# Second mixer of a two-layer decoder trunk: adaLN steps moved off the first units of two projections, two quarters of the out-projection's input made at other times

## Chip, cores and metric
The kernel runs on 1 core of one Trainium2 chip. The metric is the device time of one execution in microseconds (us). Before the change it is 2801.41 us, the median of 3 runs (2799.87 to 2802.63).

## What is computed
A trunk of two layers works on 256 tokens of width 2048, with a vector `c` of width 2048 that modulates every sub-layer (adaLN). Cut to what matters here, where layer 1 is the second layer:

```
c_act = silu(c)
for i in range(2):
    sh1, sc1, g1, sh2, sc2, g2 = split(c_act @ ada_w[i] + ada_b[i], 6)      # 2048 x 12288 weights a layer
    h = x * (1 + sc1) + sh1
    y = mixer_ab(h, ...) if i == 0 else mixer_cd(h, ...)
    x = layer_norm(ALPHA * x + (1 + g1) * y, ln1_g[i], ln1_b[i])
    h = x * (1 + sc2) + sh2
    y = (silu(h @ w_gate[i]) * (h @ w_up[i])) @ w_down[i]
    x = layer_norm(ALPHA * x + (1 + g2) * y, ln2_g[i], ln2_b[i])

mixer_cd: gb, gc, xc, q, k, v = split(h @ w_in)          # 2048 x 6144
          yc = gb * causal_dwconv(gc * xc, conv_w)       # 3 taps, 1024 channels
          yd = diff_attention(q, k, v, ...)              # 4 heads of 2 x 128
          return concatenate([yc, yd]) @ w_out           # 2048 x 2048
```

## The kernel before
**Products.** Everything is held transposed, features on the 128 partitions and the 256 tokens along the free side. Each matrix product is a list of *units*. A unit is 512 rows by 512 columns of a weight matrix, 1 MB. SyncE's queue (SP) loads it into one of four slots of `raw` (L1690), ScalarE (ACT) copies it, rounded, into `whi` (L1724), and VectorE (DVE) subtracts the two into `wlo` (L2021). Both work in two halves, and `whi` and `wlo` have two places, so the split of unit u+2 waits until TensorE (PE) has used unit u. The activation is split in the same way into `ahi` and `alo`. PE then runs three matmuls for each pair of tiles (hi x hi, lo x hi, hi x lo: L2499, L2501, L2503), 48 a unit. Four units, one for each quarter of the 2048 rows, make a group of 512 columns; the groups alternate between two halves of PSUM.

The products of the second mixer are `in1a` (k, v and q columns: 3 bodies of 8 units, the first written out, the others a loop), `in1b` (the other columns: 24 units, written out) and `out1` (the out-projection: 16 units, whose quarters are taken in the order 2, 3, 0, 1: first the two that attention makes, then the two of the short convolution).

**Order.** Each engine's program is written out by hand, and each works through it in order. The function `product` has one version for each of DVE, ACT and PE, and calls `before` and `after` at each unit j. DVE's version does, at unit j: the steps of the adaLN sum that the table `ADA_AT` (L50) names for this j, then `before`, then the split of unit u+2 (`split_lo`), then the evacuation of a finished group, then `ada_take` where `ADA_TAKE` (L66) says so, then `after`. For a product named in `BEHIND_NORM` (L53), in the body that is written out, `before` comes ahead of the steps, and these go by `ADA_BEHIND_NORM` (L54) where it has an entry for the product's shape.

**adaLN steps.** The modulation of later sub-layers is summed beside the products. A *step* is one load of 512 rows by 512 columns of `ada_w` (1 MB, issued by GpSimd, POOL, L1637) into one of two slots of `ada_units`, and four DVE instructions that add its four tiles, scaled by `c_act`, to `ada_acc` (L2000, L2003). A load is issued when its slot has been used. Four steps make a block; PE then adds over the partitions with four small matmuls (`ada_sum`, L2466) behind the unit that `ADA_SUM` (L65) names, and DVE takes the result (`ada_take`, L2009). The tables have a row for each shape of product: `(2, 8)` is `in0u` and the bodies of `in1a`, `(2, 16)` is `out1`.

**Head of in1a.** It stands behind a layer normalisation. `ln_finish` makes the first two quarters of the new activation; the rest is done at units 0 to 2 of in1a through `before` (`ln_rest`, L1840 and L2187). At unit 0 DVE subtracts, multiplies and makes `y` for the third quarter (L2136, L2141, L2147), at unit 1 it makes the third quarter of `alo` (L2154) and subtracts and multiplies for the fourth; ACT then makes eight tiles, the fourth quarter of `ahi` and `y` (L1848, L1851), and at unit 2 DVE makes the last quarter of `alo`.

**From in1b to out1.** Attention has 6 steps for each of its 4 heads, one after each unit of in1b (`attention_act`, `attention_dve`, `attention_pe`). The last result of a head is written at its step 4 by DVE (L1494). The short convolution is eight tiles of five DVE instructions (`short_conv`, L1420); four stand beside in1b (after units 13, 15, 17, 19) and four behind it. Behind in1b, `mixed_act` (L1410) waits until PE has used all units of in1b, since the mixed result goes into the same `ahi`, and copies the four quarters; `mixed_dve` (L1502) makes `alo` for three quarters, then the last four convolutions, then the last quarter. PE waits in out1 for one quarter of `alo` after the other (`mix_lo`, L2693). In out1, PE's `ln_shift` (L2571, matmul L2575) behind unit 4 waits for a sum `y` that DVE makes from the first finished group (L2076, L2077).

Of the kernel before, what the change touches and what calls it, by code (L numbers as in the profile page):

```python
# [6 lines left out]
F32 = mybir.dt.float32  # L7
F32R = mybir.dt.float32r
ALU = mybir.AluOpType
ACT = mybir.ActivationFunctionType  # L10
# [18 lines left out]
UK = 4  # L29
HALVES = 2  # L30
# [20 lines left out]
          (1, 12): [1, 1, 0, 1, 1, 0, 0, 0, 0, 0, 0, 0], (2, 8): [1, 1, 1, 1, 1, 1, 2, 0],  # L51
          (2, 16): [1, 1, 1, 1, 0, 1, 1, 1, 0, 0, 0, 1, 0, 0, 0, 0]}
BEHIND_NORM = ("up00", "up10")  # L53
ADA_BEHIND_NORM = {(1, 8): [0, 0, 0, 1, 1, 1, 1, 0]}  # L54
ROUNDS = HT // 2
# [8 lines left out]
            4: dict(shift=4, s=5, c01=5, c23=6, sq0=7, sq1=9, S=9, q01=10, S2=12, sq2=13, q2=14, root=14, fold=14)}  # L64
ADA_SUM = {(1, 8): {7: 0}, (1, 12): {6: 0}, (2, 8): {4: 0, 7: 1}, (2, 16): {4: 0, 12: 1}}  # L65
ADA_TAKE = {(1, 8): {7: 0}, (1, 12): {7: 0}, (2, 8): {5: 0, 7: 1}, (2, 16): {5: 0, 13: 1}}  # L66

# [181 lines left out]
def build(nc, x, c, ada_w, ada_b, ln1_g, ln1_b, ln2_g, ln2_b, ffn_w_gate, ffn_w_up, ffn_w_down,  # L249
# [7 lines left out]
    by_name = {p["name"]: p for p in products}  # L257

    ctx = ExitStack()
    with ctx:  # L260
# [23 lines left out]
        ahi = sb("act_hi", [P, KT, L], F32R)  # L284
        alo = sb("act_lo", [P, KT, L], F32R)
# [60 lines left out]
        tile_used = sem("tile_used")  # L346
# [43 lines left out]
        scd = Steps(sem("sc_dve"), "m c0 c1 c2 g", start=1)  # L390
        mix_hi, mix_lo = sem("mix_hi"), sem("mix_lo")
        da_setp, da_setd = Steps(sem("da_set_pool"), "nd"), Steps(sem("da_set_dve"), "gain prod lam")
        da_sete, da_seta = Steps(sem("da_set_pe"), "sum"), Steps(sem("da_set_act"), "exp")
        dad = Steps(sem("da_dve"), "s0 s1 mx0 mx1 ng r rl t0 t1 c0 c1 rr n")
# [981 lines left out]
        HEAD_UNITS = 6  # L1376

        def attention_act(act, i, j):
            h, step = j // HEAD_UNITS, j % HEAD_UNITS

            def done(ins):
# [27 lines left out]

        def mixed_act(act):  # L1410
            act.wait_ge(tile_used, HALVES * by_name["out1"]["u0"])
            for n, src in enumerate((pr1[:, Q:Q + 4], pr1[:, Q + 4:Q + 8], pr1[:, 0:4], pr1[:, 4:8])):
                if n < 2:
                    act.wait_ge(dad.sem, dad.at(2 * n + 1, "n"))
                else:
                    act.wait_ge(scd.sem, scd.at(4 * (n - 2) + 3, "g"))
                k = UK * by_name["out1"]["order"][n]
                act.activation(ahi[:, k:k + 4], src, ACT.Copy).then_inc(mix_hi, 1)

# [22 lines left out]
        def attention_dve(dve, i, j):  # L1442
            h, step = j // HEAD_UNITS, j % HEAD_UNITS

            def done(ins):
# [51 lines left out]
            if j in (13, 15, 17, 19):  # L1497
                if j == 13:
                    dve.wait_ge(grp_done, by_name["in1b"]["g0"] + 3 + 2)
                short_conv(dve, (j - 13) // 2)  # L1500

        def mixed_dve(dve):  # L1502
            def low(n, src):
                k = UK * by_name["out1"]["order"][n]
                dve.wait_ge(mix_hi, n + 1)
                dve.tensor_tensor(alo[:, k:k + 4], src, ahi[:, k:k + 4].bitcast(F32), ALU.subtract).then_inc(mix_lo, 1)
            low(0, pr1[:, Q:Q + 4])
            low(1, pr1[:, Q + 4:Q + 8])
            low(2, pr1[:, 0:4])
            dve.wait_ge(grp_done, by_name["in1b"]["g0"] + 6 + 2)  # L1510
            for t in range(4, 8):
                short_conv(dve, t)
            low(3, pr1[:, 4:8])

# [205 lines left out]
        def _(act):  # L1720
# [239 lines left out]
            product(by_name["in1b"], take(beside), after=lambda i, j: attention_act(act, i, j))  # L1960
            mixed_act(act)
            product(by_name["out1"], None, before=ln_before(2), hold=True)
            ln_finish(2)
# [15 lines left out]
        def _(dve):  # L1979
# [471 lines left out]
            dve.wait_ge(ln_gb, 8)  # L2451
            product(by_name["out1"], into_x_last(2), before=ln_before(2), hold=True)
            ln_finish(2)
# [328 lines left out]
```

## Time and profile before

| | |
|---|---|
| median of 3 runs | 2801.41 us |
| the profiled execution | 2800.32 us, span 2798.7 us |
| mean granted TensorE clock | 0.947 |
| PE busy | 2559.9 us, 91% |
| weight loads of PE | 2317.1 us, 83% |
| DVE busy | 2057.1 us, 74% |
| ACT busy | 1215.4 us, 43% |
| GpSimd busy | 197.3 us, 7% |
| chain that ended last | PE 80%, DVE 12% |

The span runs from the first to the last instruction on the core. The busy shares are means over the whole span; what a stretch is bound by is seen in the views of that stretch. A row of the timeline has start and duration in us, the engine, the line of the kernel, the operation, what it writes and reads, how many instructions are merged (x), and in brackets how long the engine had been idle and which instruction ended that.

### The profile page before, as it was taken

How to read it: one execution, taken by the hardware profiler on the slowest of the kernel's cores; microseconds unless marked ns; L12 is line 12 of the kernel's file. 1: busy time of each engine (PE TensorE's matmuls, PEld its weight loads, DVE VectorE, ACT ScalarE, POOL GpSimd, SP SyncE). 2: the span in 40 equal slices, each digit the busy share in tenths (PEclk: the TensorE clock that was granted, in tenths of full speed). 3: DMA queues.
4: the chain of work that ended last, by engine and by line, in shares of the span. 5: the costliest groups of instructions: out<-in, count | busy, mean ns of one | idle time of the engine just before them, and what ended most of it. 6: DMA issues, size and time to landing. Idle time of an engine off the chain costs nothing.

```text
span 2798.7 us, 42169 instructions
## 1 busy us (share of the span) xinstructions
PE 2559.9 (91%) x16532; PEld 2317.1 (83%) x16532; DVE 2057.1 (74%) x2594; ACT 1215.4 (43%) x1606; POOL 197.3 (7%) x226
## 2 busy tenths in 40 slices
PE   1199999888889999999999999998999999999998
PEld 1197888777887899889988889998978898899887
DVE  7788999778488777777777898568787655555556
ACT  0145556544345443444344453453454434443444
POOL 0002232100000000000001011000000000000000
PEclk6589999888899999999999999999999999999998
DMA  9863444465447888878888489555668655555552
GB/s 336 290 238 134 151 151 158 159 203 166 143 151 272 281 274 278 283 276 284 275 284 273 169 309 356 173 166 191 231 213 284 237 193 186 194 186 194 193 188 83
DMA packets 281178, 616.00 MB, mean 220 GB/s; under 512 B 23211, under 2 KB 23746, under 8 KB 280770
## 3 DMA queue, kind: packets, MB, share of 16 engines
q1 hardware_dynamic: 248386, 488.04, 51.3%
q0 software_dynamic: 32640, 125.84, 12.7%
q8 instruction: 108, 1.77, 0.2%
q14 instruction: 44, 0.36, 0.0%
HBM read 611.73 MB, written 2.10 MB: 219 GB/s over the span
## 4 chain that ended last, share of the span: by engine, by line
PE 80%; DVE 12%; issue 4%; ACT 2%; SPq 1%; DMA 1%; DVEq 0%; POOL 0%; ACTq 0%
PE groups L2499 12%; PE groups L2503 12%; PE groups L2501 12%; PE groups L2491 11%; PE groups L2495 11%; PE groups L2493 11%; PE pc L2668 1%; PE pb L2658 1%; DVE w_lo L2021 1%; PE pm L2466 1%; SPq L1644 1%; DVE ada_acc L857 1%; DVE ada_acc L2003 1%; PE groups L1116 1%; DVE xT L2141 1%
## 5 line engine op out<-in xcount | busy, mean ns | idle before, releaser
L1724 ACT ACTIVATE w_hi<-w_raw 128x1024 fp32r<-128x1024 f32 x776 | 817.0, 1059 | 1213.3 <-PE groups L2495 543.6
L2021 DVE TENSOR_TENSOR w_lo<-w_raw,w_hi 128x1024 fp32r<-128x1024 f32 x749 | 909.1, 1223 | 547.5 <-ACT w_hi L1724 543.8
L2491 PE MATMUL groups<-w_hi,act_hi 128*128 128x512 f32 x1408 | 553.5, 393 | 21.1 <-DVE act_lo L2154 21.1
L2499 PE MATMUL groups<-act_hi,w_hi 128*128 128x256 f32 x1776 | 517.5, 291 | 40.0 <-DVE act_lo L2154 13.5
L2495 PE MATMUL groups<-w_lo,act_hi 128*128 128x512 f32 x1408 | 550.1, 391 | 0.0
L2493 PE MATMUL groups<-w_hi,act_lo 128*128 128x512 f32 x1408 | 549.8, 390 | 0.0
L2501 PE MATMUL groups<-act_lo,w_hi 128*128 128x256 f32 x1776 | 509.4, 287 | 0.0
L2503 PE MATMUL groups<-act_hi,w_lo 128*128 128x256 f32 x1776 | 508.9, 287 | 0.0
L2499 PEld LDWEIGHTS groups<-act_hi,w_hi 128*128 128x128 f32 x1776 | 348.1, 196 | 52.4 <-issue 44.2
L2499 PE MATMUL groups<-hid_hi,w_hi 128*128 128x256 f32 x1392 | 388.1, 279 | 0.0
L2503 PE MATMUL groups<-hid_hi,w_lo 128*128 128x256 f32 x1392 | 386.6, 278 | 0.0
L2501 PE MATMUL groups<-hid_lo,w_hi 128*128 128x256 f32 x1392 | 386.6, 278 | 0.0
L2003 DVE SCALAR_TENSOR_TENSOR ada_acc<-ada_units,c_act,ada_acc 128x512 f32<-128x512 f32 x450 | 337.9, 751 | 19.2 <-DMA ada_units<-in_ada_w_dram 6.2
L2501 PEld LDWEIGHTS groups<-act_lo,w_hi 128*128 128x128 f32 x1776 | 348.4, 196 | 0.2
L2503 PEld LDWEIGHTS groups<-act_hi,w_lo 128*128 128x128 f32 x1776 | 347.9, 196 | 0.0
L2491 PEld LDWEIGHTS groups<-w_hi,act_hi 128*128 128x128 f32 x1408 | 265.7, 189 | 77.7 <-DVE act_lo L2154 23.6
L2495 PEld LDWEIGHTS groups<-w_lo,act_hi 128*128 128x128 f32 x1408 | 265.4, 188 | 55.9
L2493 PEld LDWEIGHTS groups<-w_hi,act_lo 128*128 128x128 f32 x1408 | 265.7, 189 | 54.3
L2501 PEld LDWEIGHTS groups<-hid_lo,w_hi 128*128 128x128 f32 x1392 | 263.0, 189 | 0.1
L2503 PEld LDWEIGHTS groups<-hid_hi,w_lo 128*128 128x128 f32 x1392 | 261.6, 188 | 0.0
L2499 PEld LDWEIGHTS groups<-hid_hi,w_hi 128*128 128x128 f32 x1392 | 261.3, 188 | 0.1
L1637 POOL DMA_DIRECT2D ada_units<-in_ada_w_dram x120 | 90.2, 751 | 1627.8 <-DVE ada_acc L2003 1373.6
(428 smaller groups left out, 2514.4 us busy)
## 6 DMA issues: line engine op xcount, KB each, us to landing
ada_units<-in_ada_w_dram POOLq DMA_DIRECT2D x120, 1024.0 KB, 6.5
w_raw<-in_ffn_w_gate_dram SPq DMA_DIRECT2D x88, 1024.0 KB, 5.2
w_raw<-in_ffn_w_up_dram SPq DMA_DIRECT2D x88, 1024.0 KB, 5.1
w_raw<-in_ffn_w_down_dram SPq DMA_DIRECT2D x88, 1024.0 KB, 5.1
w_raw<-in_cd_w_in_dram SPq DMA_DIRECT2D x48, 1024.0 KB, 5.3
w_raw<-in_ab_w_in_dram SPq DMA_DIRECT2D x40, 1024.0 KB, 5.8
ada_units<-in_ada_w_dram SPq DMA_DIRECT2D x80, 512.0 KB, 4.5
ada_first<-in_ada_w_dram SPq DMA_DIRECT2D x24, 1024.0 KB, 9.6
```

The lines of the kernel that those rows point to most:

```text
L857: last = dve.scalar_tensor_tensor(total, unit, cact[:, k:k + 1], total, ALU.mult, ALU.add)
L1116: pe.matmul(dst, whi[:, j % 2, kk, cols], ahi[:, k], start=(q == 0 and kk == 0 and t % 2 == 0), stop=False, skip_group_check=True)
L1637: engine.dma_start(aw[:, j % 2], src[UK * P * j:UK * P * (j + 1), bass.ds(col, GROUP)] .rearrange("(k p) n -> p k n", p=P)).then_inc(lande ...
L1724: act.activation(whi[:, half, k], raw[:, slot, k], ACT.Copy).then_inc(hi_done, 1)
L2003: last = dve.scalar_tensor_tensor(acc[:, b], unit[:, kk], cact[:, k:k + 1], acc[:, b], ALU.mult, ALU.add)
L2021: dve.tensor_tensor(wlo[:, half, k], raw[:, slot, k], whi[:, half, k].bitcast(F32), ALU.subtract).then_inc(lo_done, 1)
L2491: pe.matmul(dst, hi[:, k, rows], whi[:, j % 2, kk], start=(k == 0), stop=False, skip_group_check=True)
L2493: pe.matmul(dst, lo[:, k, rows], whi[:, j % 2, kk], start=False, stop=False, skip_group_check=True)
L2495: last = pe.matmul(dst, hi[:, k, rows], wlo[:, j % 2, kk], start=False, stop=(k == UK * p["units"] - 1), skip_group_check=True)
L2499: pe.matmul(dst, whi[:, j % 2, kk, cols], hi[:, k], start=(q == 0 and kk == 0 and n % 2 == 0), stop=False, skip_group_check=True)
L2501: pe.matmul(dst, whi[:, j % 2, kk, cols], lo[:, k], start=False, stop=False, skip_group_check=True)
L2503: last = pe.matmul(dst, wlo[:, j % 2, kk, cols], hi[:, k], start=False, stop=(q == p["units"] - 1 and kk == UK - 1), skip_group_check=True)
```

## The change
Four things are changed.

1. `in1a` joins `BEHIND_NORM`, and `(2, 8)` gets a row in `ADA_BEHIND_NORM`: in the written-out body of in1a, the normalisation's rest comes ahead of the steps, and the steps are 0, 0, 1, 1, 2, 2, 2, 0 for its eight units where they were 1, 1, 1, 1, 1, 1, 2, 0.
2. For shape `(2, 8)` sum and take of the first block are one unit later. This holds for in0u and all bodies of in1a.
3. In out1 the steps go from 1, 1, 1, 1, 0, 1, ... to 0, 0, 2, 1, 1, 1, ...; its sums and takes stay where they were.
4. The first mixed quarter of out1 is made during in1b, at unit 22 (ACT's copy and DVE's subtraction). Of the four convolutions behind in1b, two stay in front of out1 and two go behind unit 0 of out1, with the last quarter's copy and subtraction.

```diff
-          (2, 16): [1, 1, 1, 1, 0, 1, 1, 1, 0, 0, 0, 1, 0, 0, 0, 0]}
-BEHIND_NORM = ("up00", "up10")
-ADA_BEHIND_NORM = {(1, 8): [0, 0, 0, 1, 1, 1, 1, 0]}
+          (2, 16): [0, 0, 2, 1, 1, 1, 1, 1, 0, 0, 0, 1, 0, 0, 0, 0]}
+BEHIND_NORM = ("up00", "in1a", "up10")
+ADA_BEHIND_NORM = {(1, 8): [0, 0, 0, 1, 1, 1, 1, 0], (2, 8): [0, 0, 1, 1, 2, 2, 2, 0]}
-ADA_SUM = {(1, 8): {7: 0}, (1, 12): {6: 0}, (2, 8): {4: 0, 7: 1}, (2, 16): {4: 0, 12: 1}}
-ADA_TAKE = {(1, 8): {7: 0}, (1, 12): {7: 0}, (2, 8): {5: 0, 7: 1}, (2, 16): {5: 0, 13: 1}}
+ADA_SUM = {(1, 8): {7: 0}, (1, 12): {6: 0}, (2, 8): {5: 0, 7: 1}, (2, 16): {5: 0, 12: 1}}
+ADA_TAKE = {(1, 8): {7: 0}, (1, 12): {7: 0}, (2, 8): {6: 0, 7: 1}, (2, 16): {6: 0, 13: 1}}
@@ -1375,8 +1375,12 @@
         MQ = 51
         HEAD_UNITS = 6
 
+        MIX_AT = 22
+
         def attention_act(act, i, j):
             h, step = j // HEAD_UNITS, j % HEAD_UNITS
+            if j == MIX_AT:
+                mixed_act(act, 0)
 
             def done(ins):
                 ins.then_inc(daa.sem, 1)
@@ -1407,15 +1411,15 @@
                 on(dae_, "ss")
                 done(act.activation(dastd[:], pb[:, L:2 * L], ACT.Sqrt, scale=1.0 / (2 * P), bias=consts[:, 0:1]))
 
-        def mixed_act(act):
-            act.wait_ge(tile_used, HALVES * by_name["out1"]["u0"])
-            for n, src in enumerate((pr1[:, Q:Q + 4], pr1[:, Q + 4:Q + 8], pr1[:, 0:4], pr1[:, 4:8])):
-                if n < 2:
-                    act.wait_ge(dad.sem, dad.at(2 * n + 1, "n"))
-                else:
-                    act.wait_ge(scd.sem, scd.at(4 * (n - 2) + 3, "g"))
-                k = UK * by_name["out1"]["order"][n]
-                act.activation(ahi[:, k:k + 4], src, ACT.Copy).then_inc(mix_hi, 1)
+        def mixed_act(act, n):
+            src = (pr1[:, Q:Q + 4], pr1[:, Q + 4:Q + 8], pr1[:, 0:4], pr1[:, 4:8])[n]
+            act.wait_ge(tile_used, HALVES * (by_name["out1"]["u0"] - (1 if n == 0 else 0)))
+            if n < 2:
+                act.wait_ge(dad.sem, dad.at(2 * n + 1, "n"))
+            else:
+                act.wait_ge(scd.sem, scd.at(4 * (n - 2) + 3, "g"))
+            k = UK * by_name["out1"]["order"][n]
+            act.activation(ahi[:, k:k + 4], src, ACT.Copy).then_inc(mix_hi, 1)
 
         def short_conv(dve, t):
 
@@ -1441,6 +1445,8 @@
 
         def attention_dve(dve, i, j):
             h, step = j // HEAD_UNITS, j % HEAD_UNITS
+            if j == MIX_AT:
+                mixed_low(dve, 0)
 
             def done(ins):
                 ins.then_inc(dad.sem, 1)
@@ -1499,18 +1505,23 @@
                     dve.wait_ge(grp_done, by_name["in1b"]["g0"] + 3 + 2)
                 short_conv(dve, (j - 13) // 2)
 
+        def mixed_low(dve, n):
+            src = (pr1[:, Q:Q + 4], pr1[:, Q + 4:Q + 8], pr1[:, 0:4], pr1[:, 4:8])[n]
+            k = UK * by_name["out1"]["order"][n]
+            dve.wait_ge(mix_hi, n + 1)
+            dve.tensor_tensor(alo[:, k:k + 4], src, ahi[:, k:k + 4].bitcast(F32), ALU.subtract).then_inc(mix_lo, 1)
+
         def mixed_dve(dve):
-            def low(n, src):
-                k = UK * by_name["out1"]["order"][n]
-                dve.wait_ge(mix_hi, n + 1)
-                dve.tensor_tensor(alo[:, k:k + 4], src, ahi[:, k:k + 4].bitcast(F32), ALU.subtract).then_inc(mix_lo, 1)
-            low(0, pr1[:, Q:Q + 4])
-            low(1, pr1[:, Q + 4:Q + 8])
-            low(2, pr1[:, 0:4])
+            mixed_low(dve, 1)
+            mixed_low(dve, 2)
             dve.wait_ge(grp_done, by_name["in1b"]["g0"] + 6 + 2)
-            for t in range(4, 8):
+            for t in (4, 5):
                 short_conv(dve, t)
-            low(3, pr1[:, 4:8])
+
+        def mixed_rest(dve):
+            for t in (6, 7):
+                short_conv(dve, t)
+            mixed_low(dve, 3)
 
         def attention_set_pe(pe):
             pe.wait_ge(da_setd.sem, da_setd.at(0, "prod"))
@@ -1958,8 +1969,10 @@
                 at = HT * (g % 3) + GT * (g // 3)
                 return pr1[:, at:at + GT]
             product(by_name["in1b"], take(beside), after=lambda i, j: attention_act(act, i, j))
-            mixed_act(act)
-            product(by_name["out1"], None, before=ln_before(2), hold=True)
+            mixed_act(act, 1)
+            mixed_act(act, 2)
+            product(by_name["out1"], None, before=ln_before(2), hold=True,
+                    after=lambda i, j: mixed_act(act, 3) if j == 0 else None)
             ln_finish(2)
             ffn(1)
             ln_finish(3)
@@ -2449,7 +2462,8 @@
             mixed_dve(dve)
             gate_ready(2)
             dve.wait_ge(ln_gb, 8)
-            product(by_name["out1"], into_x_last(2), before=ln_before(2), hold=True)
+            product(by_name["out1"], into_x_last(2), before=ln_before(2), hold=True,
+                    after=lambda i, j: mixed_rest(dve) if j == 0 else None)
             ln_finish(2)
             ffn(1)
             ln_finish(3)
```

## Rows read from the trace of the kernel before

**Rows 1.** Stretches: length, busy us of PE, PEld, DVE, ACT, POOL, PEclk, DMA share, GB/s.
```profile
1616.20:1655.80 39.60, 39.28 (x305) 39.08 (x306) 35.77 (x41) 24.91 (x37) 4.60 (x7) 0.93 0.87 305
1655.80:1702.00 46.20, 46.20 (x387) 46.20 (x387) 39.31 (x48) 17.97 (x18) 5.24 (x7) 1.00 0.98 352
...
1917.00:1930.90 13.90, 13.87 (x96) 13.85 (x96) 12.10 (x24) 2.96 (x4) 0.00 (x0) 0.81 0.19 72
1935.10:1956.40 21.30, 20.46 (x156) 20.34 (x157) 20.09 (x26) 6.36 (x6) 2.24 (x3) 0.92 0.96 335
1956.40:2002.00 45.60, 45.60 (x383) 45.60 (x382) 40.59 (x49) 18.20 (x18) 2.99 (x4) 1.00 0.83 283
```

**Rows 2.** Timeline of PE in the first body of in1a.
```profile
1616.19 0.58 PE L2499 MATMUL groups<-act_hi,w_hi 128*128 128x256 f32 x1 [6.28 <-DVE act_lo L2154]
...
1625.02 0.38 PE L2499 MATMUL groups<-act_hi,w_hi 128*128 128x256 f32 x1 [0.32 <-DVE act_lo L2154]
...
1654.79 0.95 PE L2466 MATMUL pm<-ones,ada_acc 128*128 128x1 f32 x8
1655.61 0.36 PE L2499 MATMUL groups<-act_hi,w_hi 128*128 128x256 f32 x1
```

**Rows 3.** Timeline of DVE at units 0 and 1 of in1a.
```profile
1602.97 0.48 DVE L2000 TENSOR_SCALAR ada_acc<-ada_units,c_act 128x512 f32<-128x512 f32 x1
...
1605.73 1.22 DVE L2136 TENSOR_TENSOR xT<-xT,ln_stat 128x1024 f32<-128x1024 f32 x1
...
1609.54 2.35 DVE L2021 TENSOR_TENSOR w_lo<-w_raw,w_hi 128x1024 fp32r<-128x1024 f32 x2
1611.81 3.11 DVE L2003 SCALAR_TENSOR_TENSOR ada_acc<-ada_units,c_act,ada_acc 128x512 f32<-128x512 f32 x4
1614.83 1.22 DVE L2154 TENSOR_TENSOR act_lo<-y,act_hi 128x1024 fp32r<-128x1024 f32 x1
```

**Rows 4.** Timeline of ACT: the eight tiles, first and last, and what follows.
```profile
1618.48 0.60 ACT L1848 ACTIVATE act_hi<-xT,ln_fold 128x256 fp32r<-128x256 f32 x1 [6.27 <-DVE xT L2141]
...
1621.94 0.59 ACT L1851 ACTIVATE y<-xT,ln_fold 128x256 f32<-128x256 f32 x1
1622.43 1.04 ACT L1724 ACTIVATE w_hi<-w_raw 128x1024 fp32r<-128x1024 f32 x1
```

**Rows 5.** All waits of DVE from 1603 to 1656: total us, times, longest.
```profile
DVE w_lo L2021 <- ACT w_hi L1724: 2.8, 3, 1.3
```

**Rows 6.** Loads of adaLN steps: page, then issues (POOL) and uses (DVE) in the timeline.
```profile
ada_units<-in_ada_w_dram POOLq DMA_DIRECT2D x120, 1024.0 KB, 6.5
...
1642.81 0.75 POOL L1637 DMA_DIRECT2D ada_units<-in_ada_w_dram  x1 [5.27 <-DVE ada_acc L2003]
...
1645.78 6.32 DVE L2003 SCALAR_TENSOR_TENSOR ada_acc<-ada_units,c_act,ada_acc 128x512 f32<-128x512 f32 x8
...
1679.25 0.75 POOL L1637 DMA_DIRECT2D ada_units<-in_ada_w_dram  x1 [5.09 <-DVE ada_acc L2003]
...
1687.39 3.11 DVE L2003 SCALAR_TENSOR_TENSOR ada_acc<-ada_units,c_act,ada_acc 128x512 f32<-128x512 f32 x4 [0.40 <-DMA ada_units<-in_ada_w_dram]
```

**Rows 7.** Timeline of PE in out1.
```profile
1917.03 0.58 PE L2499 MATMUL groups<-act_hi,w_hi 128*128 128x256 f32 x1 [4.26 <-DVE act_lo L1506]
...
1935.12 0.35 PE L2499 MATMUL groups<-act_hi,w_hi 128*128 128x256 f32 x1 [4.04 <-DVE w_lo L2021]
...
1955.73 0.70 PE L2575 MATMUL pc<-y,ones 128*128 128x256 f32 x2 [0.82 <-DVE y L2077]
```

**Rows 8.** Timeline of DVE from the end of in1b into out1.
```profile
1913.90 1.23 DVE L2021 TENSOR_TENSOR w_lo<-w_raw,w_hi 128x1024 fp32r<-128x1024 f32 x1 [1.03 <-ACT w_hi L1724]
...
1919.17 0.42 DVE L1428 TENSOR_TENSOR sc_m<-proj 128x256 f32<-128x256 f32 x1
...
1929.65 1.23 DVE L1506 TENSOR_TENSOR act_lo<-proj,act_hi 128x1024 fp32r<-128x1024 f32 x1 [1.13 <-ACT act_hi L1418]
...
1947.53 3.12 DVE L2003 SCALAR_TENSOR_TENSOR ada_acc<-ada_units,c_act,ada_acc 128x512 f32<-128x512 f32 x4 [0.83 <-DMA ada_units<-in_ada_w_dram]
```

## Prediction, made blind

> **What bounds the kernel now.** I read the table by stretches first: TensorE (PE) is busy nearly all the time in the second mixer, but VectorE (DVE) is close behind it, 35.77 of 39.60 us in the head of in1a and 20.09 of 21.30 us in the head of out1; only the body after each head has room, 39.31 of 46.20 us [rows 1]. Then PE's timeline: two holes touch the change in in1a (6.28 and 0.32 us, both for act_lo) and three in out1 (4.26 for act_lo, 4.04 for w_lo, 0.82 for y) [rows 2, 7]. The granted clock shows what follows a hole: 0.93 over 39.60 us is 2.8 us lost at the lower level (1.2 GHz), 0.81 over 13.90 us is 2.6 us, 0.92 over 21.30 us is 1.7 us [rows 1]. The waits alone sum to 15.7 us, with the clock to 22.8 us. The last view is DVE's own: from 1603 to 1656 it waited 2.8 us in all [rows 5]. So the heads are queues of DVE work; moving one piece ahead of another only brings back what DVE or the clock really idles.
>
> Two sizes serve throughout. A unit of 48 matmuls takes PE 45.60 / 383 x 48 = 5.7 us. A step of the adaLN sum takes DVE 3.0 us (11.81 to 14.83), 2.8 when it opens a block (02.97 to 05.73), and a split of a weight unit 2.3 us (09.54 to 11.81) [rows 3].
>
> **in1a, first body.** The steps per unit go from 1,1,1,1,1,1,2,0 to 0,0,1,1,2,2,2,0, and the normalisation's rest comes ahead of them. Nothing is removed: 8 steps, the same splits, the same 4 parts of the normalisation.
> Unit 0: subtract, multiply and y take 05.73 to 09.54, 3.81 us [rows 3]; without the step ahead of them they start at 1602.97 and end at 06.8; the split follows, to 09.1. Its w_hi is no obstacle: DVE did not wait for it at 1609.54.
> Unit 1: act_lo of the third quarter is made by 10.3 instead of 16.05. PE had finished unit 1 at 1609.91 (16.19 less 6.28), so the 6.28 hole becomes 0.4 us. What is late next is the fourth quarter: subtract and multiply end at 12.6, ACT then makes eight tiles, 18.48 to 22.43 before, 3.95 us [rows 4], thus to 16.6; DVE has split unit 3 by 14.9 and idles 1.7. act_lo is there at 17.8, PE starts unit 3 at 17.9, 1.9 us after it finished unit 2.
> From there DVE has the eight steps and the splits of units 4 to 7 and half of unit 8: 6 x 3.02 + 2 x 2.78 + 4.5 x 2.27 = 33.9 us, so 1651.7 with no wait. PE began unit 8 at 1655.61 before [rows 2]. That is the most that is to be had: 3.9 us, though the first hole alone is 6.3.
> Against it stand the loads. The buffer holds two steps; a load is issued when its slot is free, some 0.65 us after, and DVE comes back to that slot after a step and a split, 5.3 us. One load took from 1679.25 to 1687.39, 8.1 us, and DVE waited for it; another, issued at 1642.81, was used in the pair that began at 1645.78 without a wait, so by 48.8, at most 6.0 us; the median of all is 6.5 [rows 6]. Two pairs follow a pair, so the wait is 2 x (0.65 + L - 5.3): 0 at L = 4.6, 3.7 at 6.5, 6.9 at 8.1. I take L = 6.25, the middle of 6.0 and 6.5, as the share of DMA is 0.87 here and 0.98 where the 8.1 was seen: 3.2 us. Unit 8 starts at 1654.9, **0.7 us earlier**; bounds 3.9 earlier and 3.0 later.
> The Trainium skill (DMA: Bandwidth & Descriptors, "Issuing engines are not separate DMA queues") says that transfers issued by different engines run on the same 16 DMA engines and interleave. The trace agrees, in that 8.1 us stands where weights and adaLN loads overlap; it speaks for the long L and against pairs of steps. By L = 8.1 the stretch would be 3.0 us slower, with no interleaving 3.9 us faster.
> Sum and take of block 0 go one unit later, in in0u as well: the same instructions (one sum is 0.95 us of PE [rows 2]) behind a unit of PE work; I cost it at nothing. If DVE's take were late, PE would wait at the next sum, two units on, for 0.15 us of work.
>
> **in1b and the head of out1.** ACT and DVE now make the first mixed quarter at unit 22. DVE idles there (1.03 us before 1913.90 [rows 8]); in front of it the last head's output comes 1 us later, which that idle takes up. Queued behind it are only the splits for out1, not needed before 1912.8. So the hole of 4.26 goes: PE enters out1 at 1912.8. The second and third quarter follow the last evacuation as all four did, 1.14 us each, by 18.1; PE needs the second at 18.5.
> Next, two short convolutions of four run in front (2.33 us each: the four of before took from 1919.17 to ACT's copy at 28.52, which is 29.65 less 1.13 [rows 8]), then the split of unit 2, 1923.0 to 25.2: PE begins unit 2 at 24.2. Then the other two, to 29.9, ACT's copy, DVE idle for 1.1 as before [rows 8], act_lo, to 32.1. ACT waits with this copy in front of unit 3's split, so w_lo of unit 3 is there at 33.3, and PE, done with unit 2 at 30.0, waits 3.4 us. Up to here PE is 8.8 us ahead (unit 3 at 33.4 against 35.12 + 5.7 + 1.4).
> It doesn't keep them. The steps were 1,1,1,1,0 and are 0,0,2,1,1, but the sum still stands behind unit 4. The chain on DVE to y, which PE waited for at 1955.73 [rows 7], holds what it held: four steps, splits of units 2 to 5, four convolutions, the residual add of the first group. Off it goes 1.14 us, the first act_lo. DVE's wait for a load before 1947.53, 0.83 us [rows 8], is replaced by that of the third step, 0.65 + L - 5.4: 0 at 4.5, 3.4 at 8.1. I take 0.75 (L = 5.5), since DVE has split little before and the queue is nearly empty (72 GB/s in the stretch ahead [rows 1]). So y is there 1.2 us earlier, 1954.5; bounds 2.0 earlier and 1.4 later. PE is done with unit 4 near 1947.3 and waits for the fourth step, whose end is some 1953: a **new hole of 5 to 6 us at the sum**. The hole of 4.26 us was followed by 2.6 us of clock loss [rows 1, 7]. In the old place such a loss lay before DVE's chain ended and cost nothing; here it lies behind it, in a stretch that PE sets (clock 1.00, 45.60 of 45.60 busy before [rows 1]). Bounds 0 and 2.8; I take 2.6. Together **1.4 us later**, bounds 2.0 earlier and 4.2 later.
> The steps from unit 4 on are the old ones, and the weight loads follow the splits, so are earlier.
>
> **Sum.** -0.7 + 1.4 = +0.7 us. The profiled execution took 2800.32 us (span 2798.7 and 1.6 around it), the median of the runs is 2801.41; on its own time the sum gives 2801.0, on the median 2802.1. I predict **2802.1 us**. Ends: -3.9 - 2.0 = 2795.5 and +3.0 + 4.2 = 2808.6.
>
> **Rivals.**
> (a) The clock does not fall behind the hole at the sum, and loads land in 5.5 us: 2801.41 - 2.2 (3.9 less a wait of 1.7 in in1a) - 1.2 = 2798.0. For it: 1.9 to 2.3 us holes stand ahead of the big one, not behind. Against: both holes above 6 us and that of 4.26 show it. 20%.
> (b) Slower: the adaLN loads decide. From L = 7 both heads lose more than they gain; at 8.1 in1a is 3.0 and out1, 1.4 + 2.6, is 4.0 later: 2808.4. For it: 0.98 of DMA in the body that follows, and 0.96 in out1's head [rows 1]; against: the pair of before with at most 6.0 us. 14%, about half of it above 2807.
> (c) The holes are worth what they measure: 15.7 - 0.4 - 1.9 - 3.4 = 10.0 us and most of the clock, 2789 or less. Against it are the 2.8 us of idle in 53 us of DVE [rows 5]; only if DVE's steps shortened could it be. 4%.
> (d) The change doesn't do what it says: ACT's copy at unit 22 waits, so the first quarter is no earlier: in1a's 0.7 alone, 2800.7. It waits for a count that unit 22 itself has reached. 2%, and inside the range.
>
> **How the numbers follow.** The forecast has 60% (2799 to 2805). The range for 8 in 10 leaves out (c), and the outer half of (b): **2797.3 to 2807.0**. No change means within 0.2%, 5.6 us, about what a measurement of this kernel can tell: 2795.8 to 2807.0. Faster is (c) and a tail of (a), 6%; slower the outer half of (b), 6%; the same, 88%.
>
> **What would show it.** Right: the hole at unit 2 of in1a under 1 us, one near 1.9 at unit 3, PE waiting at units 6 to 8 for w_lo or the sum; in out1 no hole at unit 0, some 3.4 us at unit 3, and 5 to 6 us ahead of the sum behind unit 4, with the clock below 1 after it. Unit 8 of in1a within 1655 +- 2, and the matmul of L2575 within 1 us of its old distance from it. Wrong: DVE idle in either head by over 4 us less than before, no hole at the sum, or a time outside 2795 to 2809.

## The result, and the profile after

The changed kernel takes 2819.66 us, the median of 7 runs (2812.45 to 2823.67), against 2801.41 us before. The medians differ by 18.3 us; the ratio estimated from all runs of both is 1.0056, 95% interval 1.0045 to 1.0068, which is 15.7 us, 12.6 to 19.0. The change is slower. The prediction, no change at 2802.1 and a range up to 2807.0, was wrong. Its profiled execution took 2819.66 us, span 2818.0, mean granted clock 0.943 (before 0.947).

The stretches of before, in the trace of after (same columns). The last row is new: the head and first body of in1a as a whole; the same stretch of before follows.

```profile
1616.20:1655.80 39.60, 35.35 (x252) 34.55 (x250) 31.41 (x37) 21.25 (x32) 4.05 (x6) 0.87 0.75 257
1655.80:1702.00 46.20, 39.41 (x310) 39.24 (x311) 37.16 (x46) 17.43 (x19) 5.71 (x8) 0.93 0.89 311
1917.00:1930.90 13.90, 13.90 (x116) 13.79 (x115) 7.93 (x8) 7.74 (x9) 0.00 (x0) 1.00 0.52 173
1605.00:1690.00 85.00, 73.96 (x543) 72.99 (x542) 68.30 (x85) 40.56 (x56) 8.17 (x11) 0.88 0.74 253
```
```profile
1605.00:1690.00 85.00, 78.40 (x632) 78.00 (x632) 76.60 (x92) 42.86 (x57) 9.73 (x13) 0.96 0.89 316
```

Over these 85 us DVE is busy 68.30 us instead of 76.60. No work was taken off it: it stands idle 8.3 us more (in a window moved by 6.5 us, 1611.5 to 1696.5, it is busy 68.48). The prediction had named the opposite as a sign of being wrong, DVE idle by over 4 us less; of its three signs, two came true: the time outside 2795 to 2809, and in out1 no hole at the sum.

PE's timeline, first body of in1a, then the same sum in bodies 2 and 3 (to be held against [rows 2]; L2513 is what L2499 was, L2480 what L2466 was):

```profile
1616.98 0.38 PE L2513 MATMUL groups<-act_hi,w_hi 128*128 128x256 f32 x1 [0.41 <-DVE act_lo L2167]
...
1624.74 0.38 PE L2513 MATMUL groups<-act_hi,w_hi 128*128 128x256 f32 x1 [1.75 <-DVE act_lo L2167]
...
1645.64 1.76 PE L2480 MATMUL pm<-ones,ada_acc 128*128 128x1 f32 x8 [1.90 <-DVE ada_acc L2016]
...
1656.05 0.39 PE L2513 MATMUL groups<-act_hi,w_hi 128*128 128x256 f32 x1 [0.45 <-DVE w_lo L2034]
...
1668.60 1.84 PE L2480 MATMUL pm<-ones,ada_acc 128*128 128x1 f32 x8 [6.54 <-DVE mod L2022]
...
1719.36 1.02 PE L2480 MATMUL pm<-ones,ada_acc 128*128 128x1 f32 x8 [0.64 <-DVE mod L2022]
...
1769.49 1.02 PE L2480 MATMUL pm<-ones,ada_acc 128*128 128x1 f32 x8 [2.04 <-DVE mod L2022]
```

A hole is a time in which PE stands idle. The one of 6.28 us at unit 2 is gone, and one of 6.54 stands at the second sum. The matmuls of the two traces can be set side by side one by one. PE ended unit 1 at 1616.57 (1616.98 less 0.41; before 1609.91), so 6.7 us were lost before anything in this head; the second sum is 13.8 us later (before 1654.79, [rows 2]), so 7.1 us are lost by then, and 10.9 at the end of in1a's three bodies. In out1 the shift goes down by 11 us up to unit 3 and has come back by unit 5; from unit 8 to the end of out1 it is 1.6 us above its old value.

What ended that late is read best in the chain of waits of after, cut to this stretch (start, us, what):

```profile
1633.29 9.15 DMA ada_units<-in_ada_w_dram
1642.47 0.76 DVE ada_acc L2016
...
1646.24 5.49 DMA ada_units<-in_ada_w_dram
1651.75 0.76 DVE ada_acc L2016
...
1655.51 7.46 DMA ada_units<-in_ada_w_dram
1662.99 0.76 DVE ada_acc L2016
...
1666.11 2.27 DVE w_lo L2034 x2
1668.60 1.84 PE pm L2480 x8
```

Of 35 us of this chain 22.1 are three loads: load, four DVE instructions, slot free, next load. DVE's own timeline has the waits (to be held against [rows 6]), and the place of the take:

```profile
1642.47 3.12 DVE L2016 SCALAR_TENSOR_TENSOR ada_acc<-ada_units,c_act,ada_acc 128x512 f32<-128x512 f32 x4 [4.53 <-DMA ada_units<-in_ada_w_dram]
...
1651.75 3.11 DVE L2016 SCALAR_TENSOR_TENSOR ada_acc<-ada_units,c_act,ada_acc 128x512 f32<-128x512 f32 x4 [1.13 <-DMA ada_units<-in_ada_w_dram]
...
1658.80 3.11 DVE L2016 SCALAR_TENSOR_TENSOR ada_acc<-ada_units,c_act,ada_acc 128x512 f32<-128x512 f32 x4 [1.66 <-DMA ada_units<-in_ada_w_dram]
1662.99 3.12 DVE L2016 SCALAR_TENSOR_TENSOR ada_acc<-ada_units,c_act,ada_acc 128x512 f32<-128x512 f32 x4 [1.08 <-DMA ada_units<-in_ada_w_dram]
1666.02 2.35 DVE L2034 TENSOR_TENSOR w_lo<-w_raw,w_hi 128x1024 fp32r<-128x1024 f32 x2
1668.29 0.16 DVE L2022 TENSOR_TENSOR mod<-pm,ada_b_cols 128x4 f32<-128x4 f32 x1
```

The take lasts 0.16 us and stands behind two steps and a split. PE finished unit 7 at 1662.06 and may not begin its second sum before the take. In this body, though, the take's place is only the last part of the hole: the second sum needs the eighth step too, and that ended at 1666.11, behind its late load. So of the 6.54 us some 4.1 are the late steps and 2.4 the split and the take behind them. In bodies 2 and 3 (0.64 and 2.04 us) PE waits for the take.

The four loads that DVE waited for, each in a window of its own (same columns as the stretches):

```profile
1633.30:1642.40 9.10, 9.10 (x79) 9.10 (x78) 4.54 (x6) 7.87 (x13) 1.49 (x2) 1.00 0.98 341
1646.20:1651.70 5.50, 5.50 (x27) 5.50 (x28) 4.31 (x6) 0.61 (x2) 1.19 (x2) 0.50 0.71 230
1651.30:1658.80 7.50, 7.05 (x54) 6.85 (x54) 5.28 (x7) 4.10 (x6) 1.47 (x2) 0.91 0.94 335
1655.50:1663.00 7.50, 6.11 (x49) 5.81 (x48) 4.65 (x7) 5.01 (x7) 1.18 (x2) 1.00 0.89 312
```

The longest stands where the DMA share is 0.98, the shortest where it is 0.71 (PE was at 1.2 GHz there, clock 0.50, and used weights at half the pace). The mean over the whole stretch, 0.75, shows none of this.

out1 (to be held against [rows 7]), with the changed place of y:

```profile
1951.16 0.36 PE L2513 MATMUL groups<-act_hi,w_hi 128*128 128x256 f32 x1 [3.26 <-DVE w_lo L2034]
...
1971.92 1.22 PE L2589 MATMUL pc<-y,ones 128*128 128x256 f32 x2 [5.04 <-DVE y L2090]
```

Two causes were therefore put to the test: the take's place in DVE's order, and the pairs of steps that wait for their own loads. Parts of the change were also tried alone.

### The profile page after: what moved, and what is told of

It reads as the page before. It is cut to its first block, busy times and chain, and to the rows that moved or that the text cites. A ratio compares the mean times of both kernels' runs of the same rounds, so it can differ in the third digit from the quotient of the medians.

```text
span 2818.0 us, 42172 instructions
## 1 busy us (share of the span) xinstructions
PE 2574.7 (91%) x16532; PEld 2331.0 (83%) x16532; DVE 2057.7 (73%) x2594; ACT 1218.0 (43%) x1606; POOL 197.6 (7%) x226
## 3 DMA queue, kind: packets, MB, share of 16 engines
q8 instruction: 108, 1.77, 0.2%
## 4 chain that ended last, share of the span: by engine, by line
PE 77%; DVE 12%; issue 4%; DMA 3%; ACT 3%; SPq 1%; DVEq 0%; POOL 0%; POOLq 0%; ACTq 0%
PE groups L2505 11%; PE groups L2513 11%; PE groups L2509 11%; PE groups L2507 11%; PE groups L2517 11%; PE groups L2515 11%; DMA ada_units<-in_ada_w_dram 2%; DVE ada_acc L2016 2%; PE pc L2682 1%; DVE w_lo L2034 1%; PE pb L2672 1%; PE pm L2480 1%; SPq L1655 1%; DVE ada_acc L857 1%; PE groups L1116 1%
## 5 line engine op out<-in xcount | busy, mean ns | idle before, releaser
L2513 PE MATMUL groups<-act_hi,w_hi 128*128 128x256 f32 x1776 | 521.5, 294 | 32.2 <-DVE act_lo L2288 11.4
L2513 PEld LDWEIGHTS groups<-act_hi,w_hi 128*128 128x128 f32 x1776 | 352.0, 198 | 45.3 <-issue 41.8
L2513 PE MATMUL groups<-hid_hi,w_hi 128*128 128x256 f32 x1392 | 389.3, 280 | 0.0
L2513 PEld LDWEIGHTS groups<-hid_hi,w_hi 128*128 128x128 f32 x1392 | 262.6, 189 | 0.2
```

Source lines behind the costliest of these rows:

```text
L2513: pe.matmul(dst, whi[:, j % 2, kk, cols], hi[:, k], start=(q == 0 and kk == 0 and n % 2 == 0), stop=False, skip_group_check=True)
```

## The experiments

Each was timed against the kernel before on the same chip; before was between 2801.4 and 2802.1 us each time. Ratios are to it. A loss or gain "in its trace" is how far a matmul stands from the same matmul of before, in one execution each.

| | edit | us | ratio, 95% interval |
|---|---|---|---|
| 1 | sums of (2, 8) alone | 2808.52 | 1.0016 to 1.0039 |
| 2 | in1a part with these sums | 2817.08 | 1.0044 to 1.0079 |
| 3 | out1 part alone | 2799.10 | 0.9987 to 1.0017 |
| 4 | norm ahead, old steps, old sums | 2803.83 | 0.9999 to 1.0024 |
| 5 | the change, old sums of (2, 8) | 2810.61 | 1.0015 to 1.0040 |
| 6 | as 1, take ahead of the steps | 2801.77 | 0.9993 to 1.0014 |
| 7 | as 5, small loads | 2801.31 | 0.9991 to 1.0009 |
| 8 | norm ahead, milder steps | 2804.67 | 1.0003 to 1.0020 |
| 9 | out1 part, late steps | 2798.13 | 0.9974 to 0.9995 |
| 10 | late steps alone | 2801.88 | 0.9995 to 1.0017 |
| 11 | the change, take ahead of the steps | 2808.36 | 1.0012 to 1.0033 |
| 12 | mixing moves alone | 2800.22 | 0.9986 to 1.0008 |
| 13 | as 9, sum one unit later | 2795.65 | 0.9967 to 0.9992 |
| 14 | before, small loads | 2801.96 | 0.9990 to 1.0011 |

### The parts of the change

**1. Sums alone.**
```diff
-ADA_SUM = {... (2, 8): {4: 0, 7: 1} ...
-ADA_TAKE = {... (2, 8): {5: 0, 7: 1} ...
+ADA_SUM = {... (2, 8): {5: 0, 7: 1} ...
+ADA_TAKE = {... (2, 8): {6: 0, 7: 1} ...
```
Expected: 

> The kernel before, with only the sum and the take of the first block one unit later in in0u and in1a. Theory L (the loads of bunched adaLN steps and the take that stands behind them cost the time in in1a, and the rest of the 18 us lies in stretches that the change doesn't touch): within 1.5 us of before. Rival U (the later sum in in0u costs the 6.8 us by which the changed kernel is late when in1a begins): about 7 us slower.

Measured 2808.52, 7 us slower. Theory L missed, and rival U has the size but not the place. In its trace the second sum of in0u starts at 204.18 (before 204.06) and in1a begins 1.9 us earlier than before, so the same edit in in0u shows no cost; the loss is in the three bodies of in1a, 8 us from there to the end of in1a. PE's timeline has a wait in each body that before did not have:

```profile
1654.49 1.16 PE L2466 MATMUL pm<-ones,ada_acc 128*128 128x1 f32 x8 [1.42 <-DVE mod L2009]
...
1705.19 1.02 PE L2466 MATMUL pm<-ones,ada_acc 128*128 128x1 f32 x8 [1.10 <-DVE mod L2009]
...
1756.12 1.02 PE L2466 MATMUL pm<-ones,ada_acc 128*128 128x1 f32 x8 [1.35 <-DVE mod L2009]
```
And DVE's, where the take of body 2 stands behind a step that waited for its load:
```profile
1699.59 3.11 DVE L2003 SCALAR_TENSOR_TENSOR ada_acc<-ada_units,c_act,ada_acc 128x512 f32<-128x512 f32 x4 [2.52 <-DMA ada_units<-in_ada_w_dram]
1702.62 2.35 DVE L2021 TENSOR_TENSOR w_lo<-w_raw,w_hi 128x1024 fp32r<-128x1024 f32 x2
1704.89 0.15 DVE L2009 TENSOR_TENSOR mod<-pm,ada_b_cols 128x4 f32 x1
```
The waits are 3.9 us; behind each of them some 15 matmuls run at the lower of the two clock levels. The stretch 1703 to 1711 of this kernel, then of before:
```profile
1703.00:1711.00 8.00, 6.90 (x46) 6.73 (x45) 7.03 (x10) 2.24 (x3) 0.96 (x2) 0.79 0.82 279
```
```profile
1703.00:1711.00 8.00, 8.00 (x69) 8.00 (x69) 7.21 (x10) 3.94 (x4) 0.75 (x1) 1.00 0.90 312
```
So wait and clock together make the 7 us.

**2. The in1a part** (norm ahead, steps 0, 0, 1, 1, 2, 2, 2, 0, sums as in 1); out1 as before.
Expected: 

> The in1a part alone: norm first, steps 0,0,1,1,2,2,2,0, sum and take one unit later; out1 and the mixing as before. Theory L: 10 to 12 us slower than before, as the changed kernel lost 10.9 us between the start and the end of in1a; DVE waits 8 us for loads in the first body and PE some 6 us for the take in front of the second sum. Rival O (out1's new order costs as much): at most 6 us slower.

Measured 2817.08, 15.7 us over before (6 runs), where theory L had expected 10 to 12: a miss in size, on the side away from rival O. By the end of in1a its trace is 14.1 us behind. DVE waited 10.7 us for loads from 1595 to 1755, PE 7.5 us for the take. The in1a part is the whole loss, as far as these intervals tell.

**3. The out1 part alone**; in1a and its sums as before.
Expected: 

> The out1 part alone: first mixed quarter during in1b, two convolutions and the last quarter behind unit 0, steps 0,0,2,1,1; in1a and in0u as before. Theory L: within 2 us of before, no hole at unit 0, 3.3 us at unit 3, 2.3 at unit 4, about 5 at the sum. Rival O: 6 us slower or more.

Measured 2799.10, no difference. Its trace gains 10.9 us up to unit 2 of out1, has lost them again by unit 5 and is 1.7 us behind from unit 8 to the end of out1, too little for the interval to tell.

**4. The norm ahead, nothing else.**
```diff
-BEHIND_NORM = ("up00", "up10")
+BEHIND_NORM = ("up00", "in1a", "up10")
+... (2, 8): [1, 1, 1, 1, 1, 1, 2, 0]
```
Expected: 

> The kernel before with in1a's normalisation ahead of the steps, but the steps left at 1,1,1,1,1,1,2,0 and the sums where they were. Theory L: the order is harmless and it is the bunching that costs: 1 to 2 us faster than before, holes of about 3.3 us at unit 2 and 3.1 us at unit 3 instead of 6.3 and 0.3. Rival N (norm first is itself the loss, through two holes at the lower clock): 2 us slower or more.

Measured 2803.83, not told from no change. Theory L (1 to 2 us faster) isn't borne out, and rival N (2 us slower or more) isn't excluded: the median is 2.4 us above that of before. The hole at unit 2 shrinks from 6.28 to 4.50 us and nothing comes of it in the time. So the norm's place can be little of the 18 us; the sums and the bunched steps remain.

### The take and the loads

**5. The change with the sums of (2, 8) as before.**
Expected: 

> The changed kernel with the sum and take of block 0 for shape (2, 8) put back to units 4 and 5; the norm ahead of the steps in in1a, the steps 0,0,1,1,2,2,2,0 and everything in out1 stay. Theory T (the late take stands behind two steps and a split in VectorE's order; it costs some 7 us by itself, and bunched steps that wait for their loads cost another 8 to 9): 2801.4 + 8 = 2809 to 2812, with no wait for the take longer than 0.5 us in bodies 2 and 3 of in1a. But block 0 of the first body then has only 0+0+1+1+2 = 4 steps by unit 4, so the sum behind unit 4 must wait for the pair at unit 4; T expects a hole of 4 to 8 us there in the first body only. Rival L (the sum's place is irrelevant, everything comes from the bunched steps and their loads): 2817 to 2820, as the changed kernel. Rival N (the sums are the whole loss): 2801 +- 3.

Measured 2810.61: 9 us less than the changed kernel by the medians (8 by the ratios), 8 to 9 more than before. No wait for the take is left; the sum behind unit 4 now waits for a fourth step that is late by a load, within the 4 to 8 us that theory T gave:
```profile
1640.36 1.87 PE L2480 MATMUL pm<-ones,ada_acc 128*128 128x1 f32 x8 [6.39 <-DVE ada_acc L2016]
```

**6. Experiment 1 with the take moved in DVE's order.**
```diff
+                        early = (p["ada"], p["bu"]) == (2, 8) and j == 6
+                        if early:
+                            ada_take(p["ab0"] + p["takes"][j] + p["ada"] * i)
                         for _ in range(...[p["ada"], p["bu"]][j]):
                             ada_unit(...
...
-                        if j in p["takes"]:
+                        if j in p["takes"] and not early:
```
Expected: 

> The kernel before with sum and take of block 0 one unit later for shape (2, 8) (the earlier run with the sums alone took 2808.5), and the take now ahead of the two steps and the split of its unit on VectorE. Theory T (what costs is the take's place behind two steps and a split, so that TensorE's next sum waits for it): the three waits of 1.4, 1.1 and 1.4 us at that sum and the stretches of low clock behind them go, 2801.4 +- 2. Rival S (it is the sum itself that costs at its new place, or the order of the tables in in0u): 2808 +- 2, whatever the take does. Rival W (the take, put first, makes VectorE wait for TensorE's sum, and the steps behind it are later): DVE waits for the sum by 1 us or more in each body, 2805 or more.

Measured 2801.77: the whole 7 us are back. DVE takes without a wait and then works through the steps, though the second still waits for its load:
```profile
1687.58 0.15 DVE L2009 TENSOR_TENSOR mod<-pm,ada_b_cols 128x4 f32 x1
1687.65 3.11 DVE L2003 SCALAR_TENSOR_TENSOR ada_acc<-ada_units,c_act,ada_acc 128x512 f32<-128x512 f32 x4
1693.46 3.12 DVE L2003 SCALAR_TENSOR_TENSOR ada_acc<-ada_units,c_act,ada_acc 128x512 f32<-128x512 f32 x4 [2.71 <-DMA ada_units<-in_ada_w_dram]
```
PE's sum stands behind the same unit as in experiment 1. What cost was a 0.15 us instruction behind some 11 us of others, load wait included.

**7. Experiment 5 with a quarter of each adaLN load beside in1a.**
```diff
-            engine.dma_start(aw[:, j % 2], src[UK * P * j:UK * P * (j + 1), bass.ds(col, GROUP)]
+            engine.dma_start(aw[:, j % 2, 0:n], src[UK * P * j:UK * P * j + n * P, bass.ds(col, GROUP)]
```
Expected: 

> As the run with the sums of shape (2, 8) put back, but each adaLN load beside in1a brings one tile of 128 rows instead of four (0.25 MB instead of 1 MB); VectorE does all its instructions, three of four on stale data: three quarters of the modulation summed beside in1a are left out, so the time alone is to be read. Theory T (pairs of steps wait for loads that land in up to 9 us): VectorE's waits for adaLN loads in the first body, 14.5 us in the changed kernel, fall below 2 us, and the first body ends 4 to 8 us earlier than in the run with full loads. Rival B (the bunched steps cost because VectorE has three pairs in a row between the splits, whatever the loads do): the waits for loads go, but TensorE's end of the first body moves by less than 2 us.

Measured 2801.31, 9.3 us less than experiment 5. Three quarters of what is summed beside in1a are left out, so only the time says something. DVE's waits, 1600 to 1765, in experiment 5 and here (us in total, times, longest):
```profile
DVE ada_acc L2016 <- DMA ada_units<-in_ada_w_dram: 12.0, 11, 3.3
DVE w_lo L2034 <- ACT w_hi L1735: 5.3, 8, 1.3
```
```profile
DVE w_lo L2034 <- ACT w_hi L1735: 18.1, 18, 5.5
DVE act_lo L2167 <- ACT y L1862: 1.8, 1, 1.8
```
DVE now waits for weights to split, that is, it is ahead. The hole at the sum behind unit 4 is 3.23 instead of 6.39 us.

**14. Its control: the same small loads in the kernel before.**
Expected: 

> The kernel before with the adaLN loads beside in1a cut to one tile of 128 rows instead of four; VectorE does all its instructions, three of four on stale data (three quarters of the modulation summed beside in1a are left out). It is the control for the small loads in the changed in1a, which brought 2810.6 to 2801.3. Theory T (before, VectorE waits 5 us for these loads in all of in1a's head and TensorE hardly waits for that): 2799 to 2802, so at least 7 of the 9 us belong to the bunched steps. Rival R (small loads free the queue for the weights and help any kernel): 2795 or less.

Measured 2801.96, no difference. The smaller loads bring nothing where the steps are spread; the 9 us belong to bunched steps that wait for full loads.

**11. The change with the take ahead of the steps**, by the edit of 6.
Expected: 

> The changed kernel with the take of block 0 put ahead of the steps of its unit for shape (2, 8). Theory T (the late take is worth 7 us of the 18, the bunched steps waiting for loads the rest): 2809 to 2813, no wait for the take in bodies 2 and 3 of in1a. Rival U (in the first body the steps and their loads alone keep PE waiting, the take only stands beside it; only bodies 2 and 3 gain): 2814 to 2817. Rival N (the take is everything): 2801 to 2804.

Measured 2808.36, 0.6 us under theory T's interval and 11 us less than the changed kernel by the medians (9 by the ratios). No wait for the take is left; PE waits 3.41 us for w_lo and 2.82 us for the last step in the first body, both behind late loads, as the reading of the 6.54 us above would have it.

**8. Norm ahead, with steps 0, 1, 1, 1, 1, 2, 2, 0.**
Expected: 

> The kernel before with the norm ahead of the steps in in1a and the steps of the first body 0,1,1,1,1,2,2,0 (before 1,1,1,1,1,1,2,0); sums, takes and out1 as before. Theory T: the first step goes out of the head, so the 6.28 us wait at unit 2 shrinks to about 1.5; two pairs instead of the three of the changed kernel, each second load up to 9 us; the end of the first body is 0 to 3 us earlier, 2799 to 2802. Rival B (any step moved out of the head comes back in full, with a new hole at the sum or behind): 2802 to 2805. Rival G (the head's holes are worth what they measure): 2796 or less.

Measured 2804.67, slower by 0.1% with an interval clear of 1: rival B. The hole at unit 2 is 0.60 us, but 2.55 stand at unit 3, 1.77 and 2.15 at the two sums and 1.30 at a w_lo. One step taken off the head is enough to bring its time back behind it.

### out1

**12. The mixing moves alone**, steps and sums of out1 as before.
Expected: 

> The kernel before with the mixing moves alone (first mixed quarter at unit 22, two convolutions and the last quarter behind unit 0 of out1); out1's steps 1,1,1,1,0,... and sums as before, in1a as before. Theory T (the head of out1 is VectorE's queue, only moving work past y helps): the 4.3 us wait goes and comes back as waits for w_lo at units 2 to 4 of some 4 to 7 us more; 2801.4 +- 2. Rival G (the wait at unit 0 and the clock behind it are worth what they measure): 2795 or less.

Measured 2800.22, no difference, as theory T had it. The wait of 4.26 us for act_lo is gone; one of 2.65 for w_lo is new at unit 2, and that of 4.04 at unit 3 is 3.61. From y on its trace is 2.2 us ahead:
```profile
1926.93 0.55 PE L2513 MATMUL groups<-act_hi,w_hi 128*128 128x256 f32 x1 [2.65 <-DVE w_lo L2034]
...
1939.20 0.36 PE L2513 MATMUL groups<-act_hi,w_hi 128*128 128x256 f32 x1 [3.61 <-DVE w_lo L2034]
...
1953.59 0.70 PE L2589 MATMUL pc<-y,ones 128*128 128x256 f32 x2 [0.36 <-DVE y L2090]
```

**9 and 10. Late steps**, with the mixing moves (9) and without (10).
```diff
+          (2, 16): [0, 0, 0, 1, 0, 1, 1, 1, 1, 1, 1, 1, 0, 0, 0, 0]}
+ADA_SUM = {... (2, 16): {7: 0, 12: 1}}
+ADA_TAKE = {... (2, 16): {8: 0, 13: 1}}
```
Expected of 9: 

> The kernel before with the out1 part of the change (first mixed quarter at unit 22 of in1b, two convolutions and the last quarter behind unit 0 of out1), and out1's eight steps at units 3 and 5 to 11, with the sum of block 0 behind unit 7 and its take at unit 8; in1a as before. Theory T (the 10.9 us that the out1 part gains up to unit 2 is given back because VectorE's four steps still lie ahead of y behind unit 4; VectorE has some 15 us free from 1980 to 2026): the 2.3 us wait for w_lo and the 5 us wait for y go, with the low clock behind them; 2801.4 - 7 = 2794, 2791 to 2798. Rival B (the head is a queue, whatever is deferred comes back later in out1): new waits for w_lo or the sums at units 7 to 12, 2800 to 2804. Rival G (the layer normalisation at out1's end becomes later): holes of 6.7, 1.5 and 2.0 us behind out1 grow by 3 or more, 2804 or more.

Expected of 10: 

> The kernel before with nothing but out1's steps at units 3 and 5 to 11, sum of block 0 behind unit 7, take at unit 8. Theory T: the wait of 4.0 us for w_lo at unit 3 and of 0.8 us for y go, the 4.3 us wait at unit 0 stays: 2801.4 - 5 = 2796, 2794 to 2799. Rival B: 2800 to 2804.

Measured 2798.13 for 9, at the edge of theory T's interval, and 2801.88 for 10, rival B. In 9 there is no wait for y any more, but one at the sum that was put behind unit 7, and some 26 matmuls at the lower clock around it:
```profile
1936.58 0.55 PE L2513 MATMUL groups<-act_hi,w_hi 128*128 128x256 f32 x1 [3.27 <-DVE w_lo L2034]
...
1949.63 0.59 PE L2589 MATMUL pc<-y,ones 128*128 128x256 f32 x2
...
1970.35 1.66 PE L2480 MATMUL pm<-ones,ada_acc 128*128 128x1 f32 x8 [2.86 <-DVE ada_acc L2016]
```
Experiment 10 fails at the same place: within out1 its trace is 6.2 us ahead just before this sum, waits 2.87 us there and is 0.5 behind after it. Whether it would gain with a later sum was not run.

**13. As 9, this sum behind unit 8 and its take at unit 9.**
Expected: 

> The out1 part with the late steps (units 3 and 5 to 11), sum of block 0 now behind unit 8 and its take at unit 9, one unit later than in the run that took 2798.1. In that run's trace TensorE waits 2.86 us at this sum, in the middle of 27 matmuls at the lower clock. Theory T (the wait at the sum is what is left of the head's queue, and VectorE has room behind it): wait and low clock go, 2798.1 - 4 = 2794, 2792 to 2796. Rival B (the wait moves to w_lo or to the take behind its steps): 2797 to 2800.

Measured 2795.65, 0.998 of before (0.9967 to 0.9992): the fastest kernel here, faster than before and than the change. The sum waits for nothing:
```profile
1950.53 0.59 PE L2589 MATMUL pc<-y,ones 128*128 128x256 f32 x2
...
1973.99 0.95 PE L2480 MATMUL pm<-ones,ada_acc 128*128 128x1 f32 x8
```
Deferring works in out1 because DVE has room behind y: in the trace of experiment 3 it is busy 30.79 of the 46 us from 1980 on. In in1a's first body before, it waited 2.8 us of 53 [rows 5].

## Why the prediction was wrong, step by step

**The step that failed first: "Sum and take of block 0 go one unit later ...; I cost it at nothing."** It was priced by what the take does, "0.15 us of work", and not by where it stands. DVE works in order; at unit 6 two steps and a split, some 8.3 us and a load wait, are ahead of the take, and PE's next sum is behind the unit that PE has by then nearly finished. Experiment 1 puts it at 7 us in a kernel that is otherwise that of before, and experiment 6 takes all of it away by the take's place alone. In the changed kernel the medians put it at 9 (experiment 5) to 11 us (experiment 11), the ratios at 8 to 9. That size is less sure: PE's waits for which the take's place alone is to blame are 2.4 + 0.64 + 2.04 us there, and over in1a the traces of after, 5 and 11 lose 11.0, 6.3 and 8.0 us. The Trainium skill (PSUM — Partial Sum Buffer, "Engine vs sequencer instructions") says that VectorE's queue is strictly first in, first out; the trace agrees, with 0.16 us that stand behind 8.3, and the rule, held against each moved line, would have found this one.

**The second: the load waits of in1a, taken as 2 x (0.65 + L - 5.3) with L = 6.25, 3.2 us.** The form was right and two sizes were not. Four steps wait, not two: the second step of the first pair waits as well, since its slot had come free only a split and a step before (5.3 us, and 0.65 + 9.15 - 5.3 = 4.5), and in the third pair both do. And the loads took 9.15, 5.49, 7.53 and 7.46 us, a mean of 7.4. The waits came to 4.53 + 1.13 + 1.66 + 1.08 = 8.4 us. L = 6.25 had been argued from the DMA share of the whole stretch, 0.87; over a load's own time it was 0.71 to 0.98. Experiments 5, 7 and 14 put their price at 8 to 9 us of the kernel's time. The rule that was weighed there, of the Trainium skill (DMA: Bandwidth & Descriptors, "Issuing engines are not separate DMA queues"), that the transfers of both queues share the engines, was the better guide; by the 8.1 us row the stretch was priced 3.0 later. The trace agrees in that the longest load, 9.15 us, stands at share 0.98 and the shortest, 5.49, at 0.71. At the second sum 7.1 us were lost, part of which is the take's.

**What held in in1a**: the holes of 0.4 (0.41) and 1.9 (1.75), and that the first hole is not worth its 6.3 us: with 4.50 left of it (experiment 4) or 0.60 (experiment 8) the kernel is no faster.

**out1.** Here I had misread the change: the text ahead says that its sums stay, and the prediction that "the sum still stands behind unit 4". The diff shown moves sum and take of block 0 from units 4 and 5 to 5 and 6. So the new hole isn't at the sum, which waits for nothing, but one instruction group on, at y: 5.04 us, where 5 to 6 were predicted, with 20 matmuls at the lower clock. The hole at unit 0 went as said, that at unit 3 is 3.26 (3.4), and one of 2.26 at unit 4 was not foreseen. The rest of the sum held better than the misreading deserved. PE enters out1 17.7 us later than before, and y is ready 16.2 us later (1971.9 for 1955.7): 1.5 us earlier within out1, for 1.2 predicted; experiment 3's trace has 1.5 too. Behind y some 2 us go to the lower clock (2.6 predicted) and 1 to the sum, 0.95 us, which before stood at 1953.96, ahead of the 0.82 us wait for y, and now stands behind unit 5. That nets 1.6 us later in out1 (1.7 in experiment 3), for +1.4. That the two agree so closely is partly luck, since the moved sum was not in the sum of the prediction. The time of experiment 3 can't tell so small a loss. The reason given, DVE's queue up to y, is what experiments 12, 9 and 13 bear out: a gain clear of noise came only with steps taken past y, together with the mixing moves.

**The rivals.** (b) named the right mechanism for half of the loss, but at 3.0 us in in1a where 8 to 9 were measured, and priced the whole at 2808.4; it was given 14%. No rival was about DVE's order, which is the other half; the range left no room for it.

**What stays open.** In the profiled execution of after 6.7 us are lost before in1a, in spells of lower clock near 215 to 229 and 578 to 588 us, where nothing was changed. They are not the change's: experiment 14, whose kernel is that of before up to in1a, has the same spells (granted clock 0.52 in both windows; before 0.76 and 1.00) and begins in1a 6.2 us late, while its median is that of before. Over all traces here that point lies between 5.1 us earlier and 7.5 later. The parts, 7 for the take and 8 to 9 for the load waits, make 15 to 16 us. The ratio of the changed kernel gives 15.7, so no rest is shown; by the medians' 18.3 some 2 to 3 us would be left, which these runs can't tell from noise. What each part is worth beside the other is known no better than to a few us.

## What to carry to other kernels

Price a moved instruction by what stands ahead of it in its engine's order and by who waits for it, not by its own duration: 0.15 us behind two steps and a split cost 7 us here, over three bodies. Steps that share a two-place buffer were free of waits in the head where they were spread, and waited where they were bunched: a slot came free 5.3 us before its next use, and the loads took 5.5 to 9.2. Take work off a full head only to a stretch in which the same engine has measured idle time, and move the sum that collects it along, with its take first in the order.

## What the runs showed of the hardware

1 MB loads issued by GpSimd beside the weight stream took 5.49 to 9.15 us from issue to use within 30 us of one another, where the median of the profile's page is 6.5; over a load's own time the share of the 16 DMA engines was 0.98 for the longest and 0.71 for the shortest. The share doesn't give the length by itself: in before, the load issued at 1642.81 took at most 6.0 us at a share of 0.95. A load wait of DVE does not show as a wait of PE for a load: it showed as waits for the take, for w_lo and at the sum. And short waits had a price above their length: three of 1.1 to 1.4 us each stood in some 15 matmuls at 1.2 GHz, 0.79 granted over 8 us, and cost 7 us together instead of 3.9.
